# Squares of a layer's input from its turned copy, and a new order of the first loads, in a one-core Trainium2 decoder layer

## The reference

```python
def rmsnorm(x, g):
    y = x * lax.rsqrt(jnp.mean(x * x, axis=-1, keepdims=True) + EPS)
    return y * g

def hybrid_mixer(xn, positions, w_in, ...):     # xn = rmsnorm(x, mix_norm_gain)
    h = xn @ w_in                               # 256 x 2048 @ 2048 x 5376
    ...                                         # window attention with rope, retention, w_out

x = x + hybrid_mixer(...)
x = x + memory_cross_attention(rmsnorm(x, g1), rmsnorm(mem, g2), ...)   # mem: 256 x 2048
x = x + peer_ffn(rmsnorm(x, g3), ...)           # 16384 experts of width 2048
return rmsnorm(x, final_norm_gain)
```

## Time and profile before

| | before |
|---|---|
| median of 3 runs | 1930.0 us |
| profiled execution: its own time | 1927.5 us |
| profiled execution: span | 1925.7 us |
| PE busy | 1902.2 us (99%) |
| DVE busy | 1389.7 us (72%) |
| ACT busy | 952.6 us (49%) |
| POOL busy | 1390.8 us (72%) |
| mean DMA rate | 234 GB/s |

### The profile page before, as it was taken

One profiled execution on the slowest core, in us unless ns is written; L12 is line 12 of the kernel. 1 busy time (PEld: TensorE's weight loads), 2 busy tenths in 40 slices (PEclk: granted clock), 3 DMA queues, 4 the chain that ended last, 5 costly groups with the idle time before them and its releaser, 6 DMA issues.

```text
span 1925.7 us, 35172 instructions
## 1 busy us (share of the span) xinstructions
PE 1902.2 (99%) x11794; PEld 1758.8 (91%) x11794; DVE 1389.7 (72%) x2578; ACT 952.6 (49%) x1339; POOL 1390.8 (72%) x714
## 2 busy tenths in 40 slices
PE   8999999999999999999999999999999999999997
PEld 6888889887999999999999999999999999999997
DVE  6544585046635777868888888468888879999986
ACT  6454345374544444544444444455555555555555
POOL 7866768876898999988888888985555424555611
PEclk9999999999999999999999999999999999999999
DMA  9544646654655666665665565689999988999974
GB/s 337 185 142 144 206 142 221 195 189 150 219 189 175 208 209 209 207 197 194 196 195 190 193 195 192 201 274 349 332 336 334 329 288 301 326 333 331 328 271 142
DMA packets 128235, 450.37 MB, mean 234 GB/s; under 512 B 16512, under 2 KB 19456, under 8 KB 127488
## 3 DMA queue, kind: packets, MB, share of 16 engines
q1 hardware_dynamic: 101520, 365.19, 57.0%
q0 software_dynamic: 20480, 67.13, 10.1%
q10 hardware_dynamic: 6160, 17.08, 2.5%
HBM read 445.13 MB, written 4.19 MB: 233 GB/s over the span
## 4 chain that ended last, share of the span: by engine, by line
PE 55%; POOL 32%; issue 12%; POOLq 0%; DVE 0%; DVEq 0%; ACT 0%
POOL wlo L430 32%; PE ps L1914 22%; PE ps L1817 13%; PE ps L1917 11%; PE ps L1820 7%; PE ps L1831 1%; PE ps L1893 1%; POOLq L429 0%; PE ps L1895 0%; PE ps L2004 0%; POOLq L433 0%; DVE x_back L1417 0%; DVE big L1502 0%; DVE wlo L1384 0%; DVE big L1506 0%
## 5 line engine op out<-in xcount | busy, mean ns | idle before, releaser
L430 POOL TENSOR_TENSOR wlo<-raw,whi 128x1024 fp32r<-128x1024 f32 x444 | 1076.3, 2430 | 201.3 <-ACT whi L516 186.8
L516 ACT ACTIVATE whi<-raw 128x1024 fp32r<-128x1024 f32 x436 | 461.6, 1060 | 632.9 <-PE ps L1820 358.0
L1817 PE MATMUL ps<-x_parts,whi 128*128 128x448 f32 x2048 | 589.4, 369 | 1.4 <-POOL wlo L430 1.4
L1914 PE MATMUL ps<-gate_parts,whi 128*128 128x448 f32 x1992 | 579.5, 372 | 0.0
L693 ACT ACTIVATE whi<-raw 128x1024 fp32r<-128x1024 f32 x256 | 272.3, 1064 | 300.1 <-PE ps L1917 279.1
L1820 PEld LDWEIGHTS ps<-x_parts,wlo 128*128 128x128 f32 x2048 | 384.8, 188 | 31.3
L1917 PEld LDWEIGHTS ps<-gate_parts,wlo 128*128 128x128 f32 x1992 | 374.0, 188 | 34.1
L1820 PE MATMUL ps<-x_parts,wlo 128*128 128x224 f32 x2048 | 387.1, 270 | 0.0
L1917 PE MATMUL ps<-gate_parts,wlo 128*128 128x224 f32 x1992 | 375.6, 269 | 0.0
L1384 DVE TENSOR_TENSOR wlo<-raw,whi 128x1024 fp32r<-128x1024 f32 x248 | 303.8, 1225 | 72.3 <-ACT whi L693 70.7
L1817 PEld LDWEIGHTS ps<-x_parts,whi 128*128 128x128 f32 x2048 | 310.3, 191 | 1.8 <-ACT big L647 1.1
(11 more groups left out here) (252 smaller groups left out, 2218.3 us busy)
## 6 DMA issues: line engine op xcount, KB each, us to landing
raw<-in_w_u SPq DMA_DIRECT2D x256, 512.0 KB, 3.4
raw<-in_w_v SPq DMA_DIRECT2D x256, 512.0 KB, 4.9
raw<-in_w_front SPq DMA_DIRECT2D x180, 512.0 KB, 3.5
big<-in_x_t ACTq DMA_DIRECT2D x4, 512.0 KB, 9.3
big<-in_x ACTq DMA_DIRECT2D x4, 512.0 KB, 6.4
big<-in_mem ACTq DMA_DIRECT2D x4, 512.0 KB, 5.3
big<-in_mem_t ACTq DMA_DIRECT2D x2, 1024.0 KB, 6.3
big<-in_x ACTq DMA_DIRECT2D x2, 1024.0 KB, 6.1
```

The costliest lines, as they stand in the source:

```text
L430: nc.gpsimd.tensor_tensor(wlo[:, j % SPL, :], raw[:, j % RAW, :], whi[:, j % SPL, :], ALU.subtract).then_inc(lo_done, 1)
L516: nc.scalar.activation(whi[:, j % SPL, :], raw[:, j % RAW, :], ACT.Copy).then_inc(hi_done, 1)
L1817: nc.tensor.matmul(sums[:, 0:2 * TD], whi[:, s, cols], x_parts[:, :, m, 0:TD], start=m == 0, stop=False, skip_group_check=True)
L1914: nc.tensor.matmul(sums[:, 0:2 * TD], whi[:, s, cols], gate_parts[:, g].rearrange("p k t -> p (k t)"), start=False, stop=False, skip_group ...
```

## The change

The input's rows are no longer loaded. ACT squares the turned input `XT` in four parts of 4 chunks (after pieces 4 to 7), DVE adds the 16 chunks up for each token and partition (`reduce_sum` over a rearranged view), and PE adds over the partitions with two matmuls on a column of ones (after piece 10), which leaves the sums in PSUM as the variance wants them. The variance moves behind the angles in DVE's list, and the square root from after piece 9 to after piece 12.

The loads of `XT` move from ACT's queue to SP's, in five parts (chunks 0-1, 2-3, 4-7, 8-11, 12-15), each but the last ahead of one of pieces 0 to 3. Piece 0 is split in two halves by ACT and DVE in place of ACT and POOL, and chunk pair 0 is split ahead of it; PE starts when the first half of the low part is there. An activation whose result nothing reads stands first on ACT. The memory's rows come in 8 parts of 256 KB, after pieces 5 to 12. POOL's first 11 low parts are written out in place of the first turn of its loop.

```diff
+X_CHUNKS = [slice(0, 2), slice(2, 4), slice(4, 8), slice(8, 12), slice(12, 16)]
+        XT_SQ, X_SUM = at(Y_AT, DC, T), at(QAT_AT, T)
 (SP)
             for j in range(RAW):
+                m = X_CHUNKS[j]
+                sp.dma_start(XT[:, m, :], x_t[:, m, :]).then_inc(xT_in[j], 16)
                 sp.dma_start(raw[:, j, :], w_front[j]).then_inc(raw_in[j], 16)
+            sp.dma_start(XT[:, X_CHUNKS[RAW], :], x_t[:, X_CHUNKS[RAW], :]).then_inc(xT_in[RAW], 16)
 (POOL)
-            with pool.Fori(0, POOL_END // BODY) as i:
+            pool.wait_ge(lo_done, 1)
+            for j in range(1, BODY):
+                rest_of(0, j)
+            with pool.Fori(1, POOL_END // BODY) as i:
 (ACT)
-            for q in range(4):
-                act.dma_start(XT[:, 4 * q:4 * q + 4, :], x_t[:, 4 * q:4 * q + 4, :]).then_inc(xT_in[q], 16)
+            act.wait_ge(warm_ready, 1)
+            nc.scalar.activation(stats[:, UNREAD:UNREAD + 1], WARM[:, 0:1], ACT.Copy)
-            def load_rows(k):
-                tb, cols = k // 2, slice(k % 2 * 1024, (k % 2 + 1) * 1024)
-                act.dma_start(Y[:, tb, cols], x[0, tb * P:(tb + 1) * P, cols]).then_inc(x_in[tb], 16)
             def load_memory_rows(k):
-                tb, cols = k // 2, slice(k % 2 * 1024, (k % 2 + 1) * 1024)
+                tb, cols = k // 4, slice(k % 4 * 512, (k % 4 + 1) * 512)
-            def square_x(tb):
-                act.wait_ge(x_in[tb], 32)
-                square_sum(Y[:, tb, :], N_X + tb, at(QAT_AT, D))
+            def square_x(q):
+                m = slice(4 * q, 4 * q + 4)
+                nc.scalar.activation(XT_SQ[:, m, :], XT[:, m, :], ACT.Square).then_inc(xt_squared, 1)
+            split_high(A_X, 0)
+            act.wait_ge(raw_in[0], 16)
+            nc.scalar.activation(whi[:, 0, 0:PW // 2], raw[:, 0, 0:PW // 2], ACT.Copy).then_inc(hi_half, 1)
+            nc.scalar.activation(whi[:, 0, PW // 2:], raw[:, 0, PW // 2:], ACT.Copy).then_inc(hi_done, 1)
 (DVE)
             def variances(which):
+                if which == N_X:
+                    dve.wait_ge(x_sums_out, 1)
+                    sums = ps[:, 6, 0:TB]
...
-            for b in range(8):
+            split_low(A_X, 0)
+            for part, ready, done in ((slice(0, PW // 2), hi_half, lo_half), (slice(PW // 2, PW), hi_done, lo_done)):
+                dve.wait_ge(ready, 1)
+                nc.vector.tensor_tensor(wlo[:, 0, part], raw[:, 0, part], whi[:, 0, part], ALU.subtract).then_inc(done, 1)
+            for b in range(1, 8):
                 split_low(A_X, b)
-            variances(N_X)
+            nc.vector.memset(stats[:, ONE:ONE + 1], 1.0)
+            dve.wait_ge(xt_squared, 4)
+            nc.vector.reduce_sum(X_SUM, XT_SQ.rearrange("p m t -> p t m"), AX).then_inc(x_summed, 1)
...                                                        (the angles)
+            variances(N_X)
             inverse_rms(1, N_X)
 (PE)
+                if n:
+                    pe.wait_ge(lo_done, n + 1)
+                else:
+                    pe.wait_ge(lo_half, 1)
...
+                        if n == 0 and tb == 0 and c == 1:
+                            pe.wait_ge(lo_done, 1)
+            def x_sums(_):
+                pe.wait_ge(x_summed, 1)
+                for tb in range(TB):
+                    ins = nc.tensor.matmul(ps[:, 6, tb:tb + 1], X_SUM[:, tb * P:(tb + 1) * P], stats[:, ONE:ONE + 1], start=True, stop=True)
+                ins.then_inc(x_sums_out, 1)
+PE_POINTS[10] = [("xs", 0)]
 (ACT_POINTS)
-for _b in range(8):
+for _b in range(1, 8):
     _act(_b // 2, ("x", _b))
-for _b in range(4):
-    _act(2 + _b, ("load_rows", _b))
-    _act(7 + _b, ("load_memory_rows", _b))
-for _n, _s in ((6, ("load_ident", 0)), (6, ("square_x", 0)), (7, ("square_x", 1)), (9, ("root_x", 0)),
+for _b in range(8):
+    _act(5 + _b, ("load_memory_rows", _b))
+for _q in range(4):
+    _act(4 + _q, ("square_x", _q))
+for _n, _s in ((6, ("load_ident", 0)), (12, ("root_x", 0)),
```

More of the change, by code:

```diff
@@ L173 @@
 LAST_SS = 76
-SPARSE_R = 233
+SPARSE_R, ONE = 233, 234
 TOP = 80
@@ L320, in hymba_layer @@
         xr_in = [sem(f"xr_in{i}") for i in range(TB)]
-        x_in, mem_in = [sem(f"x_in{i}") for i in range(TB)], [sem(f"mem_in{i}") for i in range(TB)]
-        xT_in, memT_in = [sem(f"xT_in{i}") for i in range(4)], [sem(f"memT_in{i}") for i in range(2)]
+        mem_in = [sem(f"mem_in{i}") for i in range(TB)]
+        xT_in, memT_in = [sem(f"xT_in{i}") for i in range(5)], [sem(f"memT_in{i}") for i in range(2)]
+        hi_half, lo_half = sem("hi_half"), sem("lo_half")
         const_in, keys_in = sem("const_in"), sem("keys_in")
@@ L338, in hymba_layer @@
         squares, var_ready, root_ready = sem("squares"), sem("var_ready"), sem("root_ready")
+        xt_squared, x_summed, x_sums_out = sem("xt_squared"), sem("x_summed"), sem("x_sums_out")
         diag_ready, rb_ready, rb_out, rescaled = sem("diag_ready"), sem("rb_ready"), sem("rb_out"), sem("rescaled")
@@ L521, in split_high @@
                     act.wait_ge(gain_in, 16)
-                    act.wait_ge(xT_in[b // 2], 16)
+                    act.wait_ge(xT_in[b if b < 2 else b // 2 + 1], 16)
                 elif v != A_X2:
@@ L559, in exps @@
                 ins.then_inc(exp_out, 1)
-            def square_x(tb):
-                act.wait_ge(x_in[tb], 32)
-                square_sum(Y[:, tb, :], N_X + tb, at(QAT_AT, D))
+            def square_x(q):
+                m = slice(4 * q, 4 * q + 4)
+                nc.scalar.activation(XT_SQ[:, m, :], XT[:, m, :], ACT.Square).then_inc(xt_squared, 1)
             def square_mem(tb):
-                act.wait_ge(mem_in[tb], 32)
+                act.wait_ge(mem_in[tb], 64)
                 square_sum(at(MEM_AT, TB, D)[:, tb, :], N_MEM + tb, at(QAT_AT, D))
@@ L634, in _ @@
                   "root_x2": lambda _: root(9, VAR + N_X2, ROOT + N_X2, 2), "exp_table": exp_table,
-                  "sines": sines, "load_rows": load_rows, "load_ident": load_ident, "load_memory_rows": load_memory_rows,
+                  "sines": sines, "load_ident": load_ident, "load_memory_rows": load_memory_rows,
                   "load_memory": load_memory, "gates": gates, "load_x": load_x,
                   "load_keys": load_keys, "cross_exps": cross_exps, "store_x2": store_x2, "store_x2t": store_x2t}
+            split_high(A_X, 0)
+            act.wait_ge(raw_in[0], 16)
+            nc.scalar.activation(whi[:, 0, 0:PW // 2], raw[:, 0, 0:PW // 2], ACT.Copy).then_inc(hi_half, 1)
+            nc.scalar.activation(whi[:, 0, PW // 2:], raw[:, 0, PW // 2:], ACT.Copy).then_inc(hi_done, 1)
             for j in range(U0):
-                high(j)
+                if j:
+                    high(j)
                 for what, k in ACT_POINTS.get(j, ()):
@@ L810, in variances @@
             def variances(which):
-                dve.wait_ge(squares, which + 2)
-                nc.vector.tensor_scalar(stats[:, VAR + which:VAR + which + 2], stats[:, SS + which:SS + which + 2], 1.0 / D, EPS,
-                                        ALU.mult, ALU.add).then_inc(var_ready, 1)
+                if which == N_X:
+                    dve.wait_ge(x_sums_out, 1)
+                    sums = ps[:, 6, 0:TB]
+                else:
+                    dve.wait_ge(squares, which)
+                    sums = stats[:, SS + which:SS + which + 2]
+                nc.vector.tensor_scalar(stats[:, VAR + which:VAR + which + 2], sums, 1.0 / D, EPS, ALU.mult, ALU.add).then_inc(var_ready, 1)
             def inverse_rms(count, which, scratch=None):
@@ L1535, in rows_piece @@
             def rows_piece(n, c0, width, last_chunk, banks, at_chunk=0, half_done=None, midway=()):
-                pe.wait_ge(lo_done, n + 1)
+                if n:
+                    pe.wait_ge(lo_done, n + 1)
+                else:
+                    pe.wait_ge(lo_half, 1)
                 s = n % SPL
@@ L1670, in r_out @@
                 ins.then_inc(ret_o, 1)
-            do = {"qk": qk_transposes, "s": head_scores, "pt": p_transposes, "o": head_outputs, "rt": r_transposes,
+            def x_sums(_):
[3 more added lines that the diff above has]
+                ins.then_inc(x_sums_out, 1)
+            do = {"xs": x_sums, "qk": qk_transposes, "s": head_scores, "pt": p_transposes, "o": head_outputs, "rt": r_transposes,
                   "ri": r_inner, "rs": r_state, "ro": r_out, "rb": lambda _: inverse_by_token(1, ps[:, 7, 0:T])}
@@ L2038, in _act @@
     ACT_POINTS.setdefault(n, []).extend(steps)
+for _b in range(1, 8):
+    _act(_b // 2, ("x", _b))
 for _b in range(8):
-    _act(_b // 2, ("x", _b))
-for _b in range(4):
-    _act(2 + _b, ("load_rows", _b))
-    _act(7 + _b, ("load_memory_rows", _b))
-for _n, _s in ((6, ("load_ident", 0)), (6, ("square_x", 0)), (7, ("square_x", 1)), (9, ("root_x", 0)),
+    _act(5 + _b, ("load_memory_rows", _b))
+for _q in range(4):
+    _act(4 + _q, ("square_x", _q))
+for _n, _s in ((6, ("load_ident", 0)), (12, ("root_x", 0)),
```

## The result

The changed kernel takes 1935.86 us (median of 20 executions, 1930.84 to 1940.32) against 1931.62 for the kernel before on the same chip (20 executions, 1929.5 to 1934.3): 1.0021 of its time, interval 1.0015 to 1.0027. Forecast were 1929.4 us and no measurable change; the measured time lies outside the range, on the slow side.

A forecast was written before the change was run, and what follows sets the result against it. PE was taken to bound the kernel, nearly without gaps behind tile 0. The terms summed to 1927.5 - 0.9 + 0.35 = 1927.0 us for the profiled execution; on the median 1930.0 - 0.55, 1929.4 us, range 1925.8 to 1931.8.

The forecast's parts named there:

- What bounds the kernel: PE, busy 1902.2 of 1925.7 us, nearly gapless behind tile 0; a start change is worth its shift at piece 7.
- the loads: Input loads at the start, on one queue: chunks 0-1 land at 4.2 us, the last chunks at 13.6.
- the first piece: Start of tile 0: PE's first matmul at 6.95 us in place of 9.51, 2.55 us sooner.
- what is left at piece 7: End of tile 0: shared DVE and POOL path leaves piece 7 at 31.0, 0.95 us sooner than 31.95; 0.9 taken.
- What is added: Two one-column matmuls on PE after piece 10 cost 0.35 us; DVE's sum of 4.85 us makes PE wait for nothing.
- What moves behind it: Tile 1: square root ends near 43, holding high part 13 back 1.0 us; covered, and moved loads cost nothing.
- a cover of 0.5: Least slack, in us, before low parts delayed by the later root make PE wait, around pieces 14 and 16.
- the slow sum: Rival: DVE's sum over chunks, 1024 bytes apart, takes up to 19.4 us; PE loses about 10, 1940 us; chance 0.06.
- The clock did not fall behind the pause: Rival: clock falls in the 2.4 us pause ahead of piece 4, costing 1.4 us, 1930.8 us; chance 0.12.
- The head start was not kept: Rival: PE runs gapless from piece 1, piece 7 at 27.5, 4.4 us sooner; 1925.9 us; chance 0.16.
- The sum: Total of all terms: 1927.0 us for an execution like the profiled one, 2.5 below the median; 1929.4 on the median.

The follow-up runs named there:

- q4: Changed kernel with every first-table gather held to an even pace and the squares laid out two chunks side by side: 1926.66 us, 0.9983 of the kernel before.
- q1: Kernel before with every gather of the first table held to an even pace: 1926.63 us, 0.9979 of the kernel before.
- c2: The changed kernel timed again with nothing altered: 1933.98 us, 1.0011 of the kernel before.
- c1: The kernel before timed again with nothing altered: 1933.10 us, 1.0004 of the kernel before beside it.
- q3: Kernel before with only the new loads and split first piece, squares from rows, and gathers at an even pace: 1926.51 us, 0.9980 of the kernel before.

## Why the prediction was wrong

*What bounds the kernel, the loads, the first piece, what is left at piece 7:* right for the profiled execution. PE started at 6.94 (forecast 6.95), piece 3 at 17.26 (17.0), piece 4 at 22.24 after a pause of 2.04 (22.3 after 2.4), piece 7 1.17 us sooner (0.95). The chunk behind a low part was the limit, as worked out. I had taken 0.50 of the clock for the first matmuls; the rows of these stretches read 1.00, but the matmuls come 0.43 us apart until 10.49, the spacing I had for 0.50; so those rows do not fit, and I go by the spacing. Piece 0 took 4.53 us (4.1 forecast). Two small terms had no working that gives them: 0.58 us for half a high part (ACT's two halves start 0.54 apart, 5.44 and 5.98), and piece 0's end, where 6.95 and its twelve matmuls make 11.1 and not 11.05; neither matters to the sum. That piece 7 came so near is in part luck: in four other profiles with the new loads it comes later than 31.95.

*What is added:* the one-column matmuls cost 0.36 us (41.77 to 42.13; forecast 0.35). The sum was the mis-sized term: 7.67 us for a forecast of 4.85. Line 1003 was the wrong row: it reads neighbours. Most of the error was hidden at first: the chunks ended at 26.7 and not at 29.4, the sum began at 27.42, 2.0 us sooner than forecast, and ended 0.8 us late.

*What moves behind it:* this step failed. I let the variance wait for PE's sums alone (42.4) and asked of the angles only that they make the sines. But the variance stands behind the angles in DVE's list, so every us of the sum moves the root and with it high part 13. With the 2.2 us that a low part cost the first conversion, which was not in the sum either, the root came at 44.63; high part 13 was held 2.7 us against a cover of 0.5. Sum and low part share the blame: the angles end at 44.45 for a forecast of 41.6, 2.2 of it the low part. I also followed tile 0 to its deadline and not tile 1, whose work the late root pushed to the edge.

*The rivals:* the slow sum is what happened, with the wrong point from which it decides: I wrote 8.5 us, by the sines. In q4, behind a sum of 4.42, the variance has its turn 0.99 us ahead of PE's sums; so with one low part sat out, as there, the root is later from about 5.4 us on. The Trainium skill's sentence against the change was right, and at 0.06 I gave it too little. The clock did not fall behind the pause in the profiled execution, but it did in 4 of 10, at the price that rival gave, 1.4 us; its chance of 0.12 was too low, and that a pause of 1.2 us had cost nothing said little of one of 2 (nor does the row given for it show what followed: it is of the pause itself). The head start was not kept in the medians. In the profile of q4's shortest execution 0.9 us of it lasts to the end, against q1's.

*The sum:* "1927.0 for an execution like the profiled one" took that execution for a typical one. It lacked the loss in the last product that most have, and I carried the 2.5 us to the median as a constant. That median, 1930.0 of three, was itself 1.6 us under the one of 20 (1931.62), which is a quarter of the 6.5 us between forecast and result. Of the 4.9 us between the two profiled executions (1932.36 and 1927.5) 1.1 are the front, 3.4 the last product, 0.4 lie outside the span.

With the gathers even, the change costs 2.4 us: about 1.9 in its short executions (1928.0 against 1926.1, the lowest of each), the rest from the long ones. With pairs in place of single elements the change is worth nothing that shows, in either direction; the forecast's sum, 0.55 us under, is within the noise of that. Whether the changed kernel loses more than the old one in the last product, with the gathers as they were, stays open: the medians' difference of 4.2 us in the first comparison and 2.4 with the even pace leave up to 2 us for it or for noise (c2 was 2.7 over the kernel before beside it, and 0.9 over c1). So does which part of the transfer makes the raw piece late.

The best kernels here are q1, q3 and q4, 0.17 to 0.21% under the kernel before; what they share is the even pace of the gathers, not the change.

## What to carry to other kernels

Price a reduction by a row with the same access, not by its element count; lay at least two of the elements side by side, on the writer's and on the reader's side. When a wait moves down a list, follow everything between its old and its new place: here the variance inherited the sum, the angles and each low part that a short instruction sat out. A pause that costs nothing in one execution can cost the clock in the next: look at several traces before calling it free. And before pricing a fraction of a per cent from one trace, see how far executions of the same kernel differ, and where.

## What the runs showed of the hardware

- DVE's sum over 4096 float32: 7.67 us with each element alone (1024 bytes apart), 4.42 in pairs 2048 bytes apart, 4.41 side by side. ACT's 1024 squares: 1.04 us written side by side, 1.12 to 1.13 with a step of 8 bytes, 1.95 to 1.99 with 64.
- A DVE instruction of 0.15 us takes 2.35 when it meets a low part of POOL (2.4 us).
- ACT's table load for the root ran at 40.36, ahead of the wait for the variance; the root followed at 44.63.
- Behind a pause of PE of 1.8 to 2.05 us in the first 26 us the granted clock fell to 0.50 in 4 profiles and stayed at 1.00 in 6; the fall cost 1.4 to 1.6 us.
- Twelve gathers or more, 1.35 to 1.5 us apart, with the DMA near 400 GB/s, were followed by a wait of ACT of 6.7 to 8.8 us for one raw piece in 8 of 10 profiles, wherever the burst lay; in the seven profiles with one gather in about 2.1 us there was none.
